# The merge behind the mLSTM recurrence as seven block products for pairs of column blocks (Strassen's scheme in Winograd's form)

## What is computed

```python
gate_a, gate_b, gate_c = jnp.split(jax.nn.sigmoid(gates), 3, axis=-1)      # gates: 3 x 1024 columns of h @ w_in
merged = gate_a * (y_a @ p['w_pa']) + gate_b * (y_b @ p['w_pb']) + gate_c * (y_c @ p['w_pc'])
return merged @ p['w_out'], (st_a, st_b, *st_c)
# y_c = sigmoid(o_pre) * layer_norm(h_f + flip(h_b)) * norm_w : needs the whole mLSTM recurrence
```

## Time and profile before

| | us |
|---|---|
| median of three runs | 1398.76 |
| the runs | 1398.65, 1398.76, 1401.52 |
| span of the profiled execution, first to last instruction | 1395.3 |
| TensorE busy (91% of the span) | 1273.1 |
| VectorE, ScalarE, GpSimd busy | 602.3, 281.4, 74.9 |
| mean granted TensorE clock | 0.963 |

### The profile page before, as it was taken

The page is one execution under the profiler, slowest core; times in us unless marked ns, Lnnn a source line. Parts: engine busy times, 40 slices in busy tenths (PEclk is TensorE's granted clock), DMA queues, the critical chain, the costliest instruction groups (busy, mean ns, idle before and its releaser), DMA issues. The chain is left out here.

```text
span 1395.3 us, 15093 instructions
## 1 busy us (share of the span) xinstructions
PE 1273.1 (91%) x5783; PEld 745.4 (53%) x5783; DVE 602.3 (43%) x1340; ACT 281.4 (20%) x577; POOL 74.9 (5%) x124
## 2 busy tenths in 40 slices
PE   3899999787989899998999999999999899799775
PEld 1455555454557777755566655555446734344332
DVE  5230566668503333434555551111197734244225
ACT  2201454254033322421111110000001011011002
POOL 0000000000000000000000000000120122122110
PEclk9999999997999899998999999999999999899998
DMA  9533234331201300203222112821433899999946
GB/s 376 220 124 125 83 121 151 121 89 27 98 21 37 97 10 18 76 11 111 91 61 61 46 53 84 261 71 46 173 125 158 321 364 419 420 420 418 421 180 256
DMA packets 64972, 221.98 MB, mean 159 GB/s; under 512 B 21390, under 2 KB 32286, under 8 KB 48254
## 3 DMA queue, kind: packets, MB, share of 16 engines
q1 hardware_dynamic: 59566, 209.39, 40.3%
q0 software_dynamic: 5184, 10.50, 2.0%
q10 hardware_dynamic: 144, 1.05, 0.2%
HBM read 211.52 MB, written 17.78 MB: 164 GB/s over the span
## 5 line engine op out<-in xcount | busy, mean ns | idle before, releaser
L503 PE MATMUL bank<-hT,ring 128*128 128x512 f32 x320 | 165.3, 598 | 0.0
L2739 PE MATMUL bank<-ew,xgT 128*64 128x512 f32 (+2 forms) x544 | 131.0, 624 | 17.8 <-DMA ew<-in_experts 15.9
L1688 PE MATMUL bank<-hT,w_ab 128*128 128x512 f32 x256 | 133.3, 603 | 4.3 <-DMA w_ab<-in_merge 3.9
L960 PE MATMUL bank<-hT,ring 128*128 128x512 f32 x192 | 100.7, 606 | 2.2 <-DVE yA L1460 2.2
L504 PEld LDWEIGHTS bank<-hT,ring 128*128 128x128 f32 x320 | 60.8, 190 | 76.5 <-issue 76.5
L2739 PEld LDWEIGHTS bank<-ew,xgT 128*64 128x64 f32 (+2 forms) x544 | 48.0, 145 | 98.0 <-issue 95.7
L1689 PEld LDWEIGHTS bank<-hT,w_ab 128*128 128x128 f32 x256 | 49.2, 192 | 62.4 <-issue 62.4
L2753 PE MATMUL bank<-ew,hidT 128*64 128x512 f32 (+2 forms) x272 | 66.7, 618 | 7.5 <-DMA ew<-in_experts 6.3
L2111 PE MATMUL bank<-w_out,mT 128*128 128x512 f32 x160 | 70.9, 604 | 2.2 <-PEq L1609 2.2
L1786 PE MATMUL bank<-hT,w_c 128*128 128x512 f32 x128 | 65.5, 594 | 0.0
L961 PEld LDWEIGHTS bank<-hT,ring 128*128 128x128 f32 x192 | 37.1, 193 | 47.2 <-issue 47.2
(11 more groups left out here) (462 smaller groups left out, 2042.5 us busy)
## 6 DMA issues: line engine op xcount, KB each, us to landing
ew<-in_experts SPq DMA_DIRECT2D x96, 1024.0 KB, 27.1
ring<-in_blocks SPq DMA_DIRECT2D x10, 2048.0 KB, 8.8
mhalf<-in_mods SPq DMA_DIRECT2D x16, 1024.0 KB, 4.9
w_ab<-in_merge SPq DMA_DIRECT2D x16, 768.0 KB, 4.5
mstage<-in_mods SPq DMA_DIRECT2D x3, 2048.0 KB, 18.0
w_c<-in_merge SPq DMA_DIRECT2D x8, 768.0 KB, 4.4
w_out<-in_w_out SPq DMA_DIRECT2D x1, 4096.0 KB, 12.3
rows<-mod_rows SPq DMA_DIRECT2D x8, 512.0 KB, 8.0
```

The source lines that it names most:

```text
L503: pe.matmul(lat[:, :], w, hT[:, k, P:T], start=(k == 0), stop=(k == KD - 1))
L960: pe.matmul(lat[:, :], w, hT[:, k, P:T], start=(k == 0), stop=(k == KD - 1))
L1688: pe.matmul(bank[5][:, :], w[:, k, :], hT[:, k, P:T], start=(k == 0), stop=(k == KD - 1))
L2739: mm = pe.matmul(bank[2 + n % 2][hs, :], xgT[:, n % 2, k, hs], ew1[w][k // 4][:, 512 * (k % 4):512 * (k % 4) + 512], start=(k == 0), stop= ...
```

## The change

- The ten units inside the turns become the eight a blocks and the first two b blocks (`SINGLE`). For the a blocks `product` writes mT without an addition.
- The other six b blocks and all eight c blocks become seven pairs (`PAIRS`): b blocks 2-3, 4-5, 6-7, then c blocks 0-1, 2-3, 4-5, 6-7. For a pair, the weights are a 2x2 matrix of blocks (two column blocks by two halves of the features), and the activations are 2x2 too (two halves of the features by two halves of the tokens, TH = 320). `seven` computes the 2x2 result by seven products in place of eight, each over 4 k-steps (gate) or 2 (projection) of one 320-token matmul, accumulating into three PSUM banks.
- The sums of weight blocks (`weight_sum`, four of 768 elements per partition for each pair) and of activations (`operand_sum`, four each: hT of 1280 elements, yB and yC of 640) are made by GpSimd, in a fixed list. The result sums are made by VectorE out of PSUM (`four`), between the products that need them.
- The weights of a pair are two transfers of 768 KB into one of two buffers w_p; the rows of the weight array are in another order. w_out keeps its place after yC; the loads of pairs 4 to 6 stand behind it, the modulation rows behind them.
- The norm is spread over pairs 0 to 2, on VectorE between the result sums and on TensorE at five places.

```diff
+    LOOP = 2 * NT
+    SINGLE = [(0, j) for j in range(KD)] + [(1, 0), (1, 1)]
+    PAIRS = [(1, 2), (1, 4), (1, 6), (2, 0), (2, 2), (2, 4), (2, 6)]
+    NPAIR, TH = len(PAIRS), T // 2
...
+    PRODUCTS = ("11", "s2", "s1", "s3", "12", "s4", "22")
...
+    g6 = Steps(nc, "merge_pairs_gpsimd", [("og",), ("h", 3), ("h", 2), ("h", 4), ("w", 0, 1), ("w", 0, 2), ("w", 0, 3), ("y", 1, 3), ("y", 1, 2), ("h", 1),
+                                          ("w", 0, 4), ("y", 1, 4), ("y", 1, 1)]
+               + [x for p in range(1, NPAIR) for x in [("w", p, m) for m in range(1, 5)] + ([("y", 2, m) for m in (3, 2, 4, 1)] if p == 4 else [])])
...
+            def load_pair(p):
+                b, j = PAIRS[p]
+                if p >= 2:
+                    sp.wait_ge(p8c.sem, p8c.after("q", p - 2, "22"))
+                elif p == 1:
+                    sp.wait_ge(a5.sem, a5.after("kw", NT - 1, 1))
+                else:
+                    sp.wait_ge(p5.sem, p5.after("qc", NT - 1, 1))
+                    sp.wait_ge(p7.sem, p7.after("proj", 7))
+                for n in range(2):
+                    sp.dma_start(w_p[p % 2][:, n, :, :].rearrange("p k m -> p (k m)"),
+                                 A["merge"][j + n][:, W_BR * b:W_BR * (b + 1)]).then_inc(got_wp[p % 2], 16)
...
+            load_pair(0)
+            load_pair(1)
+            load_pair(2)
+            load_pair(3)
             sp.wait_ge(v6.sem, v6.after("y", NT - 1))
             sp.dma_start(w_out[:], A["w_out"]).then_inc(got_wo, 16)
-            load_c(2)
+            load_pair(4)
+            load_pair(5)
+            load_pair(6)
             sp.wait_ge(mod_sent, 16)
+            sp.wait_ge(p8c.sem, p8c.after("q", 5, "22"))
...
+            def operand_sum(x, m):
+                n, src, dst = (4, hT, hx) if x == 0 else (2, (None, yB, yC)[x], yx)
+                q = lambda k, t: src[:, n * k:n * k + n, TH * t:TH * t + TH]
+                label = (("h",) if x == 0 else ("y", x))
+                if m == 3:
+                    ins = pool.tensor_tensor(dst[1][:], q(1, 1), q(0, 1), ALU.subtract)
+                elif m == 2:
+                    pool.wait_ge(g6.sem, g6.after(*label, 3))
...
+
+            def weight_sum(p, m):
+                w, s_p = w_p[p % 2], w_s[p % 2]
+                a11, a12, a21, a22 = (w[:, n, 6 * k:6 * k + 6, :] for n in range(2) for k in range(2))
+                if m == 1:
+                    pool.wait_ge(got_wp[p % 2], 32 * (p // 2 + 1))
+                    if p >= 2:
+                        pool.wait_ge(p8c.sem, p8c.after("q", p - 2, "22"))
+                    ins = pool.tensor_tensor(s_p[0][:], a21, a22, ALU.add)
+                elif m == 2:
+                    pool.wait_ge(g6.sem, g6.after("w", p, 1))
...
+                ins.then_inc(g6.step("w", p, m), 1)
+
+            pool.wait_ge(p7.sem, p7.after("proj", KD - 1))
+            for m in (3, 2, 4):
+                operand_sum(0, m)
+            pool.wait_ge(p5.sem, p5.after("qc", NT - 1, 1))
+            for m in (1, 2, 3):
+                weight_sum(0, m)
+            operand_sum(1, 3)
+            operand_sum(1, 2)
+            pool.wait_ge(p7.sem, p7.after("gate", LOOP - 1))
+            operand_sum(0, 1)
+            pool.wait_ge(p7.sem, p7.after("proj", LOOP - 1))
+            weight_sum(0, 4)
+            operand_sum(1, 4)
+            operand_sum(1, 1)
+            for p in range(1, NPAIR):
+                for m in range(1, 5):
+                    weight_sum(p, m)
+                if p == 4:
+                    pool.wait_ge(p8c.sem, p8c.after("q", 2, "22"))
+                    pool.wait_ge(v6.sem, v6.after("y", NT - 1))
+                    for m in (3, 2, 4, 1):
...
+                        operand_sum(2, m)
...
+            def seven(x, p, banks, first_of, n):
+
+                w, s_p = w_p[p % 2], w_s[p % 2]
+                src, sums = (hT, hx) if x == "g" else ((None, yB, yC)[PAIRS[p][0]], yx)
+                q = lambda k, t: src[:, n * k:n * k + n, TH * t:TH * t + TH]
+                moving = ("h",) if x == "g" else ("y", PAIRS[p][0])
+                o0, o1, o2 = banks
+                for name, out, start, stationary, of, made in (
+                        ("11", o0, True, w[:, 0, 0:6, :], q(0, 0), ()), ("s2", o1, True, s_p[1][:], sums[0][:], (2, 2)),
+                        ("s1", o2, True, s_p[0][:], q(0, 1), (1, 1)), ("s3", o1, False, w[:, 1, 0:6, :], sums[1][:], (3, 3)),
+                        ("12", o0, False, w[:, 0, 6:12, :], q(1, 0), ()), ("s4", o2, False, s_p[2][:], q(1, 1), (4,)),
+                        ("22", o0, True, w[:, 1, 6:12, :], sums[2][:], (None, 4))):
+                    if name == "11":
+                        pe.wait_ge(got_wp[p % 2], 32 * (p // 2 + 1))
+                        if p:
+                            pe.wait_ge(v8c.sem, v8c.after(x + "21", p - 1))
+                    elif name == "s2" and p:
+                        pe.wait_ge(v8c.sem, v8c.after(x + "_b", p - 1))
+                    elif name == "s1" and p:
+                        pe.wait_ge(v8c.sem, v8c.after(x + "12", p - 1))
+                    elif name == "s3":
+                        pe.wait_ge(v8c.sem, v8c.after(x + "_a", p))
+                    elif name == "12":
+                        pe.wait_ge(a8c.sem, a8c.after(x + "_s", p))
+                    elif name == "s4":
+                        pe.wait_ge(v8c.sem, v8c.after(x + "22", p))
+                    elif name == "22":
+                        if x == "g":
+                            pe.wait_ge(a8c.sem, a8c.after("t11", p))
+                        else:
+                            pe.wait_ge(v8c.sem, v8c.after("m11", p))
+                    if made and made[0]:
+                        pe.wait_ge(g6.sem, g6.after("w", p, made[0]))
+                    if len(made) > 1:
+                        pe.wait_ge(g6.sem, g6.after(*moving, made[1]))
+                    for k in range(n):
+                        mm = pe.matmul(out[:, 0:TH], stationary[:, first_of + k, :], of[:, k, :], start=(start and k == 0), stop=(k == n - 1),
+                                       skip_group_check=True)
+                    mm.then_inc(p8c.step(x, p, name), 1)
+                    yield
+
+            turns = [(1, "g", 6, 0), (1, "q", 6, 1), (2, "g", 1, 2), (2, "g", 6, 3), (2, "q", 6, 4)]
...
+                act.activation(q(0, 0), bank[5][:, 0:TH], ACT.Copy).then_inc(a8c.step("g_s", p), 1)
+                act.wait_ge(v8c.sem, v8c.after("g22", p))
+                act.activation(q(1, 1), q(1, 1), ACT.Tanh, scale=0.5).then_inc(a8c.step("t22", p), 1)
+                act.wait_ge(p8c.sem, p8c.after("g", p, "12"))
+                act.activation(q(0, 0), bank[5][:, 0:TH], ACT.Tanh, scale=0.5).then_inc(a8c.step("t11", p), 1)
...
+                act.activation(pr[:, 0, 0:TH], bank[6][:, 0:TH], ACT.Copy).then_inc(a8c.step("q_s", p), 1)
+                if p == 0:
+                    act.wait_ge(v6.sem, v6.after("mv", NT - 1, H - 1))
+                    act.activation(rs6[:].rearrange("p t h -> p (t h)"), mv6[:, :, :, 1].rearrange("p t h -> p (t h)"), ACT.Sqrt, bias=col(E_LN)).then_inc(a6.step("sqrt"), 1)
...
+                dst = pr[:, i % 2, :] if i >= KD else mTk(j)
...
+            def four(x, p, banks, dst, between):
+
+                o0, o1, o2 = (bk[:, 0:TH] for bk in banks)
+                q = lambda n, t: dst[:, n, TH * t:TH * t + TH]
+                dve.wait_ge(p8c.sem, p8c.after(x, p, "s2"))
+                dve.wait_ge(a8c.sem, a8c.after(x + "_s", p))
+                dve.tensor_tensor(q(0, 1), o1, q(0, 0), ALU.add).then_inc(v8c.step(x + "_a", p), 1)
+                between(0)
+                dve.wait_ge(p8c.sem, p8c.after(x, p, "s3"))
+                dve.tensor_tensor(q(1, 0), o1, q(0, 0), ALU.add).then_inc(v8c.step(x + "_b", p), 1)
+                dve.wait_ge(v8c.sem, v8c.after(x + "_b", p))
+                dve.tensor_tensor(q(1, 1), o2, q(1, 0), ALU.add).then_inc(v8c.step(x + "22", p), 1)
+                between(1)
+                dve.wait_ge(p8c.sem, p8c.after(x, p, "s4"))
+                dve.tensor_tensor(q(0, 1), o2, q(0, 1), ALU.add).then_inc(v8c.step(x + "12", p), 1)
+                between(2)
+                dve.wait_ge(p8c.sem, p8c.after(x, p, "22"))
+                dve.tensor_tensor(q(1, 0), q(1, 0), o0, ALU.subtract).then_inc(v8c.step(x + "21", p), 1)
+                between(3)
+
+            def gates_between(p):
+                def work(i):
+                    if p == 0:
...
+                    elif p == 1:
+                        if i < 3:
+                            norm(i)
+                        else:
+                            norm(3)
+                            norm(4)
+                    elif p == 2:
+                        if i == 0:
+                            gated(1)
+                        elif i == 2:
+                            gated(2)
+                return work
+
+            def projections_between(p):
```

(64 more changed lines are left out.)

203 lines of the change are left out of this document (83 added, 120 removed).

## The result

The changed kernel takes 1409.49 us (median of five runs, 1407.74 to 1414.41) where the kernel before takes 1398.76 (1397.40 to 1402.19, five runs). The ratio is 1.0081, 95% interval 1.0054 to 1.0108: slower by 7.6 to 15.1 us, 11.3 in the middle (the two medians are 10.7 apart). The forecast was +16.5, 1415.3, in a range of 1396 to 1421.

A forecast was written before the change was run, and what follows sets the result against it. Matmul columns on TensorE were taken to bound the merge's last stretch. Terms: -22.7 + 3.4 + 9.5 + 1.7 + 0.7 + 16.0 + 6.6 + 1.3 = +16.5 us on the median of 1398.76, giving 1415.3 us, range 1396 to 1421.

The forecast's parts named there:

- The saving: Seven pairs of column blocks in the merge: fewer 320-token products save 22.7 us of TensorE time.
- The first mLSTM pair: Pair 3: TensorE waits for yC sums listed behind pair 4's weight sums, whose weights land behind w_out: 16.0 us.
- The recurrence's tail: First pair's fourth product waits for g_a, queued behind a VectorE chain that GpSimd instructions interrupt: 9.5 us.
- The last turn: Last turn of the recurrence: GpSimd's three h sums delay VectorE's decay matrix, so TensorE stands for 3.4 us.
- Pair 1: VectorE's two norms and one gating between g21 and q_a make q_a end 0.7 us late.
- s4's waits: Product s4 of each pair's projection waits for q_b and q22, one after the other: 0.24 x 7 = 1.7 us.
- Restarts: Slow granted clock after each of the three long stalls: 2.2 us each, 6.6 us in all.
- The end: Before w_out's product, q21, m2 and sum1 stand behind sum0 on VectorE: 1.3 us.
- Rival A: GpSimd and VectorE do not take turns to the chain's harm; 3.4 + 9.5 and two restarts go: 1398.0 us; chance 0.17.
- rival B: Pair 4 not held up behind w_out; pair 3's stall is 1.5 us without slow restart: 1398.6 us; chance 0.08.
- C: Both Rival A and rival B hold, matmul saving nearly whole: 1381 us; chance 0.07 together with any other gain.
- D: Worse: more turns, the norms' collisions, proportional prices: +9 us at most, up to 1424; chance 0.08.

The follow-up runs named there:

- experiment 7: Changed kernel without GpSimd's sums, products taking unsummed blocks (output not the layer's): ratio 0.9859 to the kernel before, stretch 200.9 us.
- experiment 1: Changed kernel with the four yC sums ahead of pair 4's weight sums in GpSimd's list: ratio 0.9954 to the kernel before, stretch 215.1 us.
- experiment 2: Changed kernel with pair 4's load ahead of the wait for yC and of w_out: ratio 0.9981 to the kernel before, stretch 219.0 us.
- Experiment 6: As experiment 5, with GpSimd's weight sums for pair 2 waiting for VectorE's norms in pair 1: ratio 0.9876 to the kernel before, stretch 201.5 us.
- experiment 3: Changed kernel with GpSimd's three h sums waiting for VectorE's last-turn decay matrix: ratio 1.0064 to the kernel before, stretch 228.6 us.
- experiment 4: Changed kernel with all tail sums beside VectorE's chain except the h sum moved behind its end: ratio 1.0053 to the kernel before, stretch 224.9 us.
- experiment 5: Changed kernel with the edits of experiment 1, experiment 3 and experiment 4 together: 1379.64 us, ratio 0.9859 to the kernel before, stretch 202.9 us.

## Why the forecast held, point by point

- **The saving, 22.7 us.** Right, by the matmul groups and by experiment 7.
- **The first mLSTM pair, 16.0 us of stall.** Right in every link: T, when pair 2's last product has been issued, is 889.8; yC is complete at T + 4.3 (4.4 forecast), GpSimd begins on pair 4's weights at T + 20.2 (20.7), the second yC sum ends at T + 30.5 (30.9), and the wait is 13.9 (14.0). The further wait, at s1, was 0.7 in place of 1.9. Its row names VectorE's q_a, but s1 does not wait for q_a in the program; it waits for the fourth yC sum, as forecast. That sum ends at 923.40 and q_a at 923.41. In experiment 2, where the two lie apart, the same wait is put down to L1709. The size was off because s2, with the clock low, took 2.5 us for 1.1 and covered most of what I had counted. 14.5 in all. Experiments 1 and 2 show the cause. TensorE's row at T and the row of s1, and GpSimd's row of the fourth yC sum:

```profile
889.80 0.60 PE L1835 MATMUL bank<-cst,h_f 128*128 128x128 f32 x4
...
923.55 2.47 PE L1874 MATMUL bank<-yC,w_s 128*128 128x320 f32 x4 [0.67 <-DVE pr L2109]
```
```profile
921.87 1.53 POOL L1709 TENSOR_TENSOR yC<-yC 128x640 f32<-128x640 f32 x1
```

- **The recurrence's tail, 9.5 us.** The mechanism is right, the size too large: 6.2. The mis-sized term is the 14.6 us of GpSimd instructions between VectorE's steps, which came to 10.4 (15.6 - 5.2). I charged each at its full time. But GpSimd goes on while VectorE does what needs no turn, the reciprocals and the product of block 9 out of PSUM, 1.1 us, and each wait begins after the GpSimd instruction has. Measured against the times of before, six of the chain's eight steps lost 1.2 to 1.5 us each to a y or w sum or 2.7 to the h sum. The first step met a yB sum that was nearly over and lost 0.15, and the last met a w sum that was half over and lost 0.7. That is seven GpSimd instructions in between, not eight. 10.4 less the slack of 4.0 is 6.4.
- **The last turn, 3.4 us.** 2.3. VectorE's delay was 5.0, near the 5.2 forecast, but TensorE's transposes start on the first direction's half of the matrix (783.55 + 0.69 = 784.24, transposes at 784.29), and I had priced the second's, 0.6 us later.
- **Pair 1, 0.7 us.** 1.6. The step that failed is that norm stays out of the turns, which I took since no row of the kernel before showed it. Experiment 6 shows that it does not; without the sums beside it the wait is 0.4. The 2.5 us that the prediction set beside this term were too many; the wait was 0.5 to 1.9 in the profiles with the sums beside the norm.
- **s4's waits, 1.7 us.** About 2.0: in each projection s4 starts 1.27 us after the product before it and the next one 1.18 after s4, for 1.08 each.

```profile
836.82 1.24 PE L1874 MATMUL bank<-yB,w_p 128*128 128x320 f32 x4
838.09 1.34 PE L1874 MATMUL bank<-yB,w_s 128*128 128x320 f32 x4
839.27 1.24 PE L1874 MATMUL bank<-y_sum,w_p 128*128 128x320 f32 x4
```

- **Restarts, 6.6 us.** 1.9 behind the first wait (experiment 3), 1.6 behind the second (822.34 to the next product at 826.05, 3.7 for 2.15), 3.5 in pair 3's s2, s1 and s3 (2.5, 2.3 and 2.0 for 1.08 each): 7.0. That the total is so near is in part luck. I had put 2.2 on each; two were smaller, and the third was larger by what its slow s2 took off the wait at s1.
- **The end, 1.3 us.** 1.3. The modulation rows came in time: no wait.

The errors are -1.5, -3.3, -1.1, +0.9, +0.3, +0.4 and 0, and the sum of 16.5 becomes 12.2 by the terms, 11.4 by the stretch. The three large errors lean one way: the two waits in the recurrence and those of the first mLSTM pair were put too high. Rival A (no turns) is refuted by VectorE's times in the changed kernel and by experiments 3 and 4, rival B (pair 4 not behind w_out) by the 14.3 us to landing, and GpSimd's start on those weights at T + 20.2, not within 8 us; C falls with both. Of D only the norm's collisions came about, at 0.9 us of the 9.

What stays open: the 0.9 us by which the terms exceed the stretch, and the differences of up to 3 us outside the stretch between profiles of kernels that are the same there.

## What to carry to other kernels

A form of a product with fewer columns pays its full share on a TensorE that is never idle, if the sums it needs are off every path; here the same operations cost 31 us or 2 by when one engine's list lets them run. Work given to GpSimd has to be placed by what VectorE does in that time: put it beside operations that read PSUM or while VectorE waits, and keep it from a chain of small dependent steps, each of which can lose a whole GpSimd instruction. In a fixed list, read what each item waits for, and put what waits for the slowest transfer last; the item behind it waits for that transfer too.

## What the runs showed of the hardware that was not expected

The granted clock behind the same idle is not the same from profile to profile, of which there is one for each kernel. The changed kernel and experiments 1 to 7 have 3.48 to 3.50 us of idle before w_out's product, behind the same products. The mean granted clock of the 6 us after it was 0.51 in the changed kernel, 0.74, 0.51, 0.51, 0.72, 1.00, 0.74 and 0.72 in experiments 1 to 7: nothing lost in one profile, and the lower level of 1.2 GHz through nearly the whole window in three. Behind the wait of 2.3 us it was 0.72 in the three profiles of experiments 1, 2 and 4 and in the changed kernel, and 0.50 behind the 13.9 us in three of three.

Two windows of the changed kernel, behind the first wait and behind the last:

```profile
784.30:790.30 6.00, 6.00 (x21) 4.00 (x22) 1.72 (x3) 4.00 (x11) 0.00 (x0) 0.72 0.00 0
...
1003.70:1009.70 6.00, 5.96 (x7) 2.50 (x8) 0.00 (x0) 1.28 (x1) 0.00 (x0) 0.51 0.79 283
```

Norm's operation, one SBUF tensor in and one out in float32, took turns with GpSimd (5.41 us for four in place of 1.1), which I had left out for want of a row.
